# Last stage of a two-layer latent-attention and convolution backbone: the squares' sum moved to VectorE, the loads moved between the stores

## The chip, the core and the metric

The kernel runs on one core of a Trainium2 chip. The core has TensorE (matrix products into PSUM), VectorE and ScalarE (element-wise work), GpSimd, and SyncE, whose instruction stream only issues the DMA transfers here. In the rows they are PE (PEld for its weight loads), DVE, ACT, POOL and SP. The metric is the device time of one execution in microseconds, the median over several. All arithmetic is float32, with matrix products built from split high and low parts.

## The reference, cut to what matters

Two layers work on 2048 tokens of width 1024: an attention layer, then a convolution layer. The stage of this change computes the end of the second layer. `u` is the output of the depthwise convolution, `g` the gate path, `x` the stream before the layer:

```python
def layer_norm(x, g, b):
    mu = jnp.mean(xf, axis=-1, keepdims=True)
    var = jnp.mean(jnp.square(xf - mu), axis=-1, keepdims=True)
    y = (xf - mu) * lax.rsqrt(var + EPS)
    return y * g + b
...
    u = jax.nn.silu(layer_norm(u, g_ln, b_ln)) * jax.nn.silu(g)
    return u @ w_o
...
    x = x + gate_x * rms_norm(yx, g_post[i])
```

The mean and the variance run over the 1024 channels of each token.

## The kernel before, in words

The program is a row of stages: the projections of the first layer, its attention, its output, the projections and the convolution of the second layer, and last `conv_out`, from line 1762. Only `conv_out` is touched. It begins at about 2995 us of the profiled span and ends the program.

**Tiles.** `conv_out` handles the 2048 tokens as NB = 8 blocks of W = 256. A block lies with channels on the 128 partitions: KD = 8 groups of 128 channels, so `z` holds 128 x 8 x 256 numbers for it, in two halves of HK = 4 groups (1024 elements per partition each). `z` (the convolution's output) and `gt` (the silu of the gate) have two slots, `r` = 0 and 1; block number 2i + r uses slot r. The loops are written as a first pass (i = 0), a hardware loop (i = 1, 2) and a last pass (i = 3), each with two blocks.

**What a block goes through.** SyncE loads z and gt from HBM (`load_zg`, L1809, four transfers of 512 KB, issued at L1813). GpSimd adds the eight channel groups to one (`sums`, L2044 to L2046: 1024, 512, 256 elements wide). TensorE multiplies this with a matrix of ones, which sums over the partitions and gives each partition the result (`mean_sum`, L1998, one matmul that the chip runs as two instructions, since it is plain float32). ScalarE scales it to `mu` (L1857), VectorE subtracts it in two halves (`centre`, L1933), ScalarE squares the two halves into `sq` (L1861). TensorE sums the squares over channels: eight plain float32 matmuls with the ones, accumulated in `pvar` (`var_sum`, L2004, 16 instructions). ScalarE takes the root (L90), VectorE the reciprocal (L1938) and multiplies (`normalise`, L1942), ScalarE applies the silu by group (`silu_part`, L1876), GpSimd multiplies with the gate (`gate`, L2053), ScalarE rounds to the high part (`high`, L1885), VectorE takes the rest (`low`, L1949). TensorE then multiplies with the output weights: for each of two tiles of 128 tokens (u = 0, 1) and each of two halves of the output width (h = 0, 1) 24 matmuls of 512 columns (`split3`, L95 to L97). For each u, ScalarE sums the squares of the result (`stat`, L1892) and takes a root (L90), and VectorE forms the output (`residual`, L1955 reciprocal, L1957 from PSUM, L1963 adding `x`). SyncE stores it (L1845).

**The order of the work** is written out by hand, one order for each engine, and an engine takes its instructions strictly in this order. For block b (with n = b + 1 the next one):

- TensorE: group u0 h0, `var_sum(n)`, group u0 h1, group u1 h0, `mean_sum(b + 2)`, group u1 h1.
- ScalarE: `root(n)`, `silu_part(n)`, `stat(b, 0)`, `high(n)`, `mean(b + 2)` (scale, then both halves of the squares), `stat(b, 1)`.
- VectorE: `normalise(n)`, `residual(b, 0)`, `low(n)`, `centre(b + 2)`, `residual(b, 1)`.
- GpSimd: `sums(b + 2)`, `gate(n)`.
- SyncE: wait for `gate(b)`, `load_zg(b + 2)`, then for u = 0 and 1: wait for the output, store it, load the x of block n.

Ahead of the loop stand the first blocks' steps, mixed with the splitting of the eight weight groups (`weights_high`, `weights_low`, L1969). GpSimd there does `sums(0)`, `sums(1)`, `gate(0)`. `Chain` (L63) issues an instruction and waits for it on the same engine before the next.

Of the kernel before, what the change touches and what calls it, by code (L numbers as in the profile page):

```python
# [1756 lines left out]
def conv_out(nc, net):  # L1757
# [10 lines left out]
    with nc.cleanup_on_exit(), ExitStack() as st:  # L1768
# [17 lines left out]
        s_w, s_z, s_gt = net.sems("co_w_in", WR), net.sems("co_z_in", 2), net.sems("co_gt_in", 2)  # L1786
        s_x, s_st = net.sems("co_x_in", 2), net.sems("co_stored", 2)
        (s_const, s_whi, s_wlo, s_mean, s_mu, s_zc, s_sq, s_var, s_zn, s_v, s_vg, s_vhi, s_vlo, s_y, s_ss, s_tmp,
         s_out, s_rt, s_rs, s_mr, s_rr, s_zsum, s_add) = (net.sem("co_" + n) for n in (
             "const", "whi", "wlo", "mean", "mu", "zc", "sq", "var", "zn", "v", "vg", "vhi", "vlo", "y", "ss",  # L1790
             "tmp", "out", "rt", "rs", "mr", "rr", "zsum", "add"))
        block = st.enter_context(nc.Block())

        def loop(eng, body):

            body(0, True, False)
            with eng.Fori(1, NB // 2 - 1) as i:
                body(i, False, False)
            body(NB // 2 - 1, False, True)

        def nxt(i, r):
            return (i, 1) if r == 0 else (i + 1, 0)
# [6 lines left out]
        def load_zg(sp, i, r):  # L1809
            for dst, src, sem in ((z, net.z_phases, s_z), (gt, net.gate1, s_gt)):  # L1810
                for half in range(2):
                    g = slice(half * KD // 2, (half + 1) * KD // 2)
                    sp.dma_start(dst[:, r, g], src[g, :, bass.ds(i * 2 + r, 1), :].rearrange("g p a n -> p (g a) n")  # L1813
                                 ).then_inc(sem[r], 16)

        def rows(dram, i, r, u):

            return dram.rearrange("(n s) d -> s n d", s=PHASES)[bass.ds(i * 2 + r, 1), u * P:(u + 1) * P, :].rearrange(
                "a n d -> (a n) d")

        @block.sync
        def _(sp):
            def load_x(i, r, u):
                sp.dma_start(xt[:, u], rows(net.x1, i, r, u)).then_inc(s_x[u], 16)

            load_zg(sp, 0, 0)
            for dst, src in ((gln[:], net.g_ln), (bln[:], net.b_ln), (gp[:], net.gp_flat[1:2, :].to_broadcast([P, D]))):
                sp.dma_start(dst, src).then_inc(s_const, 16)
            for k in range(KD):
                if k >= WR:  # L1830
                    sp.wait_ge(s_wlo, k - WR + 1)
                sp.dma_start(wst[:, k % WR], net.w_o1[:, k]).then_inc(s_w[k % WR], 16)
            load_zg(sp, 0, 1)
            for u in range(TB):
                load_x(0, 0, u)

            def body(i, first, last):
                for r in range(2):
                    if not last:

                        sp.wait_ge(s_vg, i * 4 + 2 * (r + 1))
                        load_zg(sp, i + 1, r)
                    for u in range(TB):
                        sp.wait_ge(s_out, i * 4 + (2 * r + u + 1))
                        sp.dma_start(rows(net.out, i, r, u), ob[:, u]).then_inc(s_st[u], 16)  # L1845
                        if not (last and r):
                            load_x(*nxt(i, r), u)

            loop(sp, body)
            for u in range(2):  # L1850
                sp.wait_ge(s_st[u], 16 * NB)

        @block.scalar
        def _(act):
            def mean(i, r):
                act.wait_ge(s_mean, i * 2 + (r + 1))
                nc.scalar.activation(mu[:], pmu[:, 0:W], ACT.Copy, scale=1.0 / D).then_inc(s_mu, 1)  # L1857
                for half in range(2):
                    k = slice(half * HK, (half + 1) * HK)
                    act.wait_ge(s_zc, i * 4 + (2 * r + half + 1))  # L1860
                    nc.scalar.activation(sq[:, k], z[:, r, k], ACT.Square).then_inc(s_sq, 1)  # L1861

            def root(i, r):
                act.wait_ge(s_var, i * 2 + (r + 1))
                if not static(i, r) or r:
                    act.wait_ge(s_zn, i * 4 + 2 * r)
                root_mean(nc, net, rs[:], pvar[:, 0:W], D).then_inc(s_rt, 1)

            def silu_part(i, r):

                if not static(i, r) or r:
                    act.wait_ge(s_vlo, i * 4 + 2 * r)
                for k in range(KD):
                    if k % HK == 0:
                        act.wait_ge(s_zn, i * 4 + (2 * r + k // HK + 1))
                    nc.scalar.activation(v[:, k], z[:, r, k], ACT.Silu,  # L1876
                                         scale=gln[:, k:k + 1], bias=bln[:, k:k + 1]).then_inc(s_v, 1)

            def high(i, r):
                if not static(i, r):  # L1880
                    act.wait_ge(s_y, i * 4 + 2 * (r - 1))
                for half in range(2):
                    k = slice(half * HK, (half + 1) * HK)
                    act.wait_ge(s_vg, i * 4 + (2 * r + half + 1))
                    nc.scalar.activation(vhi[:, r, k], v[:, k], ACT.Copy).then_inc(s_vhi, 1)  # L1885

            def stat(i, r, u):
                s = 2 * r + u
                act.wait_ge(s_y, i * 4 + (s + 1))
                if not isinstance(i, int) or i:  # L1890
                    act.wait_ge(s_tmp, i * 4 + (s - 3))
                nc.scalar.activation(junk[:], ps[:, u], ACT.Square, accum_out=ss[:, s:s + 1]).then_inc(s_ss, 1)  # L1892
                act.wait_ge(s_ss, i * 4 + (s + 1))
                root_mean(nc, net, rr[:, s:s + 1], ss[:, s:s + 1], D).then_inc(s_mr, 1)

            act.wait_ge(s_const, 48)
            def weights_high(first, last):
                for k in range(first, last):
                    act.wait_ge(s_w[k % WR], 16 * (k // WR + 1))
                    nc.scalar.activation(whi[:, k], wst[:, k % WR], ACT.Copy).then_inc(s_whi, 1)  # L1900

            mean(0, 0)
            weights_high(0, 3)
            root(0, 0)
            weights_high(3, 5)
            silu_part(0, 0)
            high(0, 0)
            weights_high(5, KD)
            mean(0, 1)

            def body(i, first, last):
                for r in range(2):
                    n = None if last and r else nxt(i, r)
                    if n:
                        root(*n)
                        silu_part(*n)
                    stat(i, r, 0)
                    if n:
                        high(*n)
                    if not last:  # L1920
                        mean(i + 1, r)
                    stat(i, r, 1)

            loop(act, body)

        @block.vector
        def _(dve):
            def centre(i, r):
                dve.wait_ge(s_mu, i * 2 + (r + 1))
                dve.wait_ge(s_z[r], i * 32 + 32)  # L1930
                for half in range(2):
                    k = slice(half * HK, (half + 1) * HK)
                    nc.vector.tensor_tensor(z[:, r, k], z[:, r, k], mu[:].unsqueeze(1).to_broadcast([P, HK, W]),  # L1933
                                            ALU.subtract).then_inc(s_zc, 1)

            def normalise(i, r):
                dve.wait_ge(s_rt, i * 2 + (r + 1))
                nc.vector.reciprocal(rs[:], rs[:]).then_inc(s_rs, 1)  # L1938
                dve.wait_ge(s_rs, i * 2 + (r + 1))
                for half in range(2):  # L1940
                    k = slice(half * HK, (half + 1) * HK)
                    nc.vector.tensor_tensor(z[:, r, k], z[:, r, k], rs[:].unsqueeze(1).to_broadcast([P, HK, W]),  # L1942
                                            ALU.mult).then_inc(s_zn, 1)
# [26 lines left out]
                                            ALU.subtract).then_inc(s_wlo, 1)  # L1970

            centre(0, 0)
            weights_low(0, 3)
            normalise(0, 0)
            weights_low(3, 5)
            low(0, 0)
            weights_low(5, KD)
            centre(0, 1)

            def body(i, first, last):  # L1980
                for r in range(2):
                    n = None if last and r else nxt(i, r)
                    if n:
                        normalise(*n)
                    residual(i, r, 0)
                    if n:
                        low(*n)
                    if not last:
                        centre(i + 1, r)
                    residual(i, r, 1)  # L1990

            loop(dve, body)

        @block.tensor
        def _(pe):
# [2 lines left out]
                nc.tensor.matmul(pmu[:, 0:W], net.ones[:], zsum[:, 0], start=True, stop=True).then_inc(s_mean, 1)  # L1998

            def var_sum(i, r):  # L2000
                for k in range(KD):
                    if k % HK == 0:
                        pe.wait_ge(s_sq, i * 4 + (2 * r + k // HK + 1))
                    mm = nc.tensor.matmul(pvar[:, 0:W], net.ones[:], sq[:, k], start=(k == 0), stop=(k == KD - 1))  # L2004
                mm.then_inc(s_var, 1)

            mean_sum(0, 0)
            var_sum(0, 0)
# [185 lines left out]
```

## Time and profile before

| | us |
|---|---|
| median of 3 runs | 3262.49 |
| lowest and highest run | 3260.82, 3264.07 |
| the profiled execution's own time | 3262.19 |
| its span, from the first to the last instruction | 3260.2 |
| TensorE busy in the span | 3001.7 (92%) |
| VectorE, ScalarE, GpSimd busy | 1757.5, 1422.4, 431.0 |
| mean granted TensorE clock, share of full speed | 0.972 |

The profiled execution stands 0.3 us below the median. The busy shares are of the whole program; `conv_out` is its last 265 us, and an instruction of it is told by a name that begins with `co_`. Times of instructions are counted from the span's start. In a timeline row the columns are start, duration, engine, line, operation, output and inputs, shape, and, in brackets, the idle time of the engine before it with what ended it. Instructions of the same kind that follow each other stand as one row with their count.

### The profile page before, as it was taken

The page shows a single profiled execution, that of the slowest core. Times are in us where ns is not written, and L with a number is a line of the kernel's source. Part 1 is how long each engine was busy: PE and PEld are TensorE (multiplying, and loading weights), DVE is VectorE, ACT ScalarE, POOL GpSimd, SP SyncE. Part 2 cuts the span into 40 slices and gives each one's busy share as a digit, 9 for nine tenths or more (in the row PEclk, how much of TensorE's full clock was granted, in tenths as well). Part 3 has the DMA queues.
Part 4 walks back from the last instruction along what each step waited for, and adds up shares of the span by engine and source line. Part 5 has one row for each costly group of instructions (what it writes and reads, how often), then busy time and mean ns, then how long its engine had stood idle before and what let it go on. Part 6 is the DMA issues. An engine that isn't in the chain of part 4 may idle for free. (4 is left out here: it accounts for less than half of the span.)

```text
span 3260.2 us, 44295 instructions
## 1 busy us (share of the span) xinstructions
PE 3001.7 (92%) x15091; PEld 2495.0 (77%) x15091; DVE 1757.5 (54%) x2927; ACT 1422.4 (44%) x2971; POOL 431.0 (13%) x285
## 2 busy tenths in 40 slices
PE   2999999699999999999999998996899999997798
PEld 2878878588888878787878886784688888886677
DVE  6654554366766666767676765435233323333554
ACT  3554545356555655555555554325111111112543
POOL 1000000010111111110111110003011111112331
PEclk9999999899999999999999999997899999998899
DMA  6546455511112121211111100533222222213443
GB/s 219 182 158 228 147 178 182 174 51 44 51 33 69 40 70 40 69 36 44 50 55 54 40 27 29 203 127 123 71 70 70 65 68 73 70 54 125 134 155 103
DMA packets 217944, 308.07 MB, mean 94 GB/s; under 512 B 81008, under 2 KB 142720, under 8 KB 216576
## 3 DMA queue, kind: packets, MB, share of 16 engines
q1 hardware_dynamic: 213120, 296.98, 28.0%
q10 hardware_dynamic: 4608, 8.39, 0.7%
q8 instruction: 114, 1.87, 0.2%
q14 instruction: 102, 0.84, 0.1%
HBM read 213.94 MB, written 91.37 MB: 94 GB/s over the span
## 5 line engine op out<-in xcount | busy, mean ns | idle before, releaser
L1086 ACT ACTIVATE at_prob<-at_S,at_nmax 128x512 f32<-128x512 f32 (+1 forms) x640 | 411.4, 659 | 371.6 <-DVE at_nmax L1200 367.8
L1223 DVE TENSOR_TENSOR at_ptlo<-at_T,at_pthi 128x512 fp32r<-128x512 f32 x576 | 396.7, 689 | 319.4 <-ACT at_pthi L1102 318.3
L1102 ACT ACTIVATE at_pthi<-at_T 128x512 fp32r<-128x512 f32 x576 | 349.2, 609 | 225.4 <-PE at_T L972 225.4
L1189 DVE TENSOR_REDUCE at_mx<-at_S 128x1 f32<-128x512 f32 (+1 forms) x640 | 393.6, 630 | 84.2 <-PE at_S L946 77.4
L972 PE MATMUL at_T<-ident,at_prob 128*128 128x128 f32 x2304 | 345.8, 272 | 3.2 <-DVE at_ptlo L1223 3.2
L972 PEld LDWEIGHTS at_T<-ident,at_prob 128*128 128x128 f32 x2304 | 278.3, 140 | 69.4 <-DVE at_ptlo L1223 16.6
L95 PE MATMUL ci_ps<-h1hi,ci_whi 128*128 128x512 f32 x768 | 300.1, 391 | 17.6 <-DVE ci_wlo L1651 17.6
L96 PE MATMUL ci_ps<-h1lo,ci_whi 128*128 128x512 f32 x768 | 299.8, 390 | 0.0
L97 PE MATMUL ci_ps<-h1hi,ci_wlo 128*128 128x512 f32 x768 | 299.7, 390 | 0.0
L941 PE MATMUL at_S<-at_khi,at_qhi 128*128 128x512 f32 (+1 forms) x640 | 249.7, 390 | 48.6 <-ACT at_prob L1086 25.8
L95 PE MATMUL at_O<-at_pthi,at_vhi 128*128 128x512 f32 x576 | 272.8, 474 | 0.6 <-DVE at_og L1232 0.5
L516 DVE TENSOR_TENSOR fr_wlo<-fr_w,fr_whi 128x1024 fp32r<-128x1024 f32 (+1 forms) x99 | 114.6, 1160 | 250.0 <-ACT fr_whi L388 249.9
L945 PE MATMUL at_S<-at_krhi,at_qr 128*128 128x512 f32 (+1 forms) x640 | 238.7, 373 | 0.0
L943 PE MATMUL at_S<-at_khi,at_qlo 128*128 128x512 f32 (+1 forms) x640 | 238.0, 372 | 0.0
L946 PE MATMUL at_S<-at_krlo,at_qr 128*128 128x512 f32 (+1 forms) x640 | 237.7, 371 | 0.0
L942 PE MATMUL at_S<-at_klo,at_qhi 128*128 128x512 f32 (+1 forms) x640 | 237.4, 371 | 0.0
L97 PE MATMUL at_O<-at_pthi,at_vlo 128*128 128x512 f32 x576 | 227.6, 395 | 0.0
L96 PE MATMUL at_O<-at_ptlo,at_vhi 128*128 128x512 f32 x576 | 227.5, 395 | 0.0
L1607 ACT ACTIVATE ci_sig<-ci_ps 128x512 f32<-128x512 f32 x64 | 38.3, 598 | 429.1 <-PE ci_ps L97 429.1
L1658 DVE TENSOR_TENSOR ci_ub<-ci_ps,ci_sig 128x512 f32<-128x512 f32 x32 | 35.0, 1094 | 330.5 <-PE ci_ps L97 330.5
L1317 POOL TENSOR_TENSOR at_gden<-at_den,at_gst 128x512 f32<-128x512 f32 x32 | 41.4, 1294 | 1196.9 <-ACT at_den L1102 1196.9
L1752 POOL TENSOR_TENSOR ci_blo<-ci_tlo,ci_mask 128x640 fp32r<-128x640 f32 x64 | 109.0, 1712 | 604.4 <-DVE ci_tlo L1675 417.2
(202 smaller groups left out, 6391.9 us busy)
## 6 DMA issues: line engine op xcount, KB each, us to landing
fr_w<-in_w_front SPq DMA_DIRECT2D x75, 512.0 KB, 4.1
at_wmod<-in_w_mod SPq DMA_DIRECT2D x32, 512.0 KB, 3.3
ci_w<-in_cv_w_in SPq DMA_DIRECT2D x24, 512.0 KB, 4.2
fr_w<-in_w_front SPq DMA_DIRECT2D x24, 384.0 KB, 3.9
values<-fr_ob SPq DMA_DIRECT2D x36, 256.0 KB, 2.9
at_kst<-k_nope SPq DMA_DIRECT2D x8, 1152.0 KB, 7.3
at_vst<-values SPq DMA_DIRECT2D x8, 1152.0 KB, 7.3
fr_x<-in_x SPq DMA_DIRECT2D x16, 512.0 KB, 6.6
```

What stands on the lines that cost most here:

```text
L95: nc.tensor.matmul(out, whi, xhi, start=first, stop=False)
L96: nc.tensor.matmul(out, whi, xlo, start=False, stop=False)
L97: return nc.tensor.matmul(out, wlo, xhi, start=False, stop=last)
L941: nc.tensor.matmul(out, qhi[:, r, q], khi[:, k], start=True, stop=False)
L943: nc.tensor.matmul(out, qlo[:, r, q], khi[:, k], start=False, stop=False)
L945: nc.tensor.matmul(out, qr[:, r, q], krhi[:, k], start=False, stop=False)
L946: nc.tensor.matmul(out, qr[:, r, q], krlo[:, k], start=False, stop=True).then_inc(s_qk, 1)
L972: mm = nc.tensor.transpose(out[:, i * P:(i + 1) * P], prob[:, j % 2, i, kt * P:(kt + 1) * P], net.ident[:])
L1086: nc.scalar.activation(prob[:, j % 2, i, k], S[:, c, 0:k.stop - k.start], ACT.Exp, scale=SCALE, bias=nmax[:, i % 2:i % 2 + 1], accum_out=l ...
L1102: nc.scalar.activation(dst, T[:, (n + SLOTS * j) % 2], ACT.Copy).then_inc(s_hi, 1)
L1189: nc.vector.tensor_reduce(mx[:, i % 2, c:c + 1], S[:, c, 0:k.stop - k.start], AXX, ALU.max).then_inc(s_mx, 1)
L1223: nc.vector.tensor_tensor(ptlo[:, kt % 3], T[:, (n + SLOTS * j) % 2], pthi[:, kt % 3].bitcast(F32), ALU.subtract).then_inc(s_lo, 1)
```

## The change

The sum of the squares over channel groups moves from TensorE to VectorE: a new function `square_sums` adds the eight groups of `sq` in place in three steps, and `var_sum` becomes one matmul on the result. VectorE does it at the end of a block's list, after `residual(b, 1)`, for block b + 2. ScalarE gets a wait for the variance matmul of the block before, ahead of squaring. In the weights' order, VectorE splits two groups ahead of `square_sums(0, 0)` instead of three.

SyncE's list is written out flat over the eight blocks. Block 2's z and gt are loaded ahead of all stores, once `gate(0)` is done. After the first store (u = 0) of block b, and the x load behind it, SyncE waits for `gate(b + 1)` and loads z and gt of block b + 3.

```diff
-            def body(i, first, last):
-                for r in range(2):
-                    if not last:
-
-                        sp.wait_ge(s_vg, i * 4 + 2 * (r + 1))
-                        load_zg(sp, i + 1, r)
-                    for u in range(TB):
-                        sp.wait_ge(s_out, i * 4 + (2 * r + u + 1))
-                        sp.dma_start(rows(net.out, i, r, u), ob[:, u]).then_inc(s_st[u], 16)
-                        if not (last and r):
-                            load_x(*nxt(i, r), u)
-
-            loop(sp, body)
+            sp.wait_ge(s_vg, 2)
+            load_zg(sp, 1, 0)
+            for b in range(NB):
+                i, r = b // 2, b % 2
+                for u in range(TB):
+                    sp.wait_ge(s_out, i * 4 + (2 * r + u + 1))
+                    sp.dma_start(rows(net.out, i, r, u), ob[:, u]).then_inc(s_st[u], 16)
+                    if b + 1 < NB:
+                        load_x(*nxt(i, r), u)
+                    if u == 0 and b + 3 < NB:
+                        sp.wait_ge(s_vg, 2 * (b + 2))
+                        load_zg(sp, (b + 3) // 2, (b + 3) % 2)
...
                     act.wait_ge(s_zc, i * 4 + (2 * r + half + 1))
+                    if half == 0 and not (static(i, r) and r == 0):
+                        act.wait_ge(s_var, i * 2 + r)
                     nc.scalar.activation(sq[:, k], z[:, r, k], ACT.Square).then_inc(s_sq, 1)
...
+            def square_sums(i, r):
+                dve.wait_ge(s_sq, i * 4 + (2 * r + 2))
+                link = Chain(dve, s_sqadd, i * 4 + 2 * r)
+                link(nc.vector.tensor_tensor(sq[:, 0:HK], sq[:, 0:HK], sq[:, HK:KD], ALU.add))
+                link(nc.vector.tensor_tensor(sq[:, 0:HK // 2], sq[:, 0:HK // 2], sq[:, HK // 2:HK], ALU.add))
+                nc.vector.tensor_tensor(sq[:, 0], sq[:, 0], sq[:, 1], ALU.add).then_inc(s_sqsum, 1)
...
             centre(0, 0)
-            weights_low(0, 3)
+            weights_low(0, 2)
+            square_sums(0, 0)
+            weights_low(2, 3)
             normalise(0, 0)
             weights_low(3, 5)
             low(0, 0)
             weights_low(5, KD)
             centre(0, 1)
+            square_sums(0, 1)
...
                     residual(i, r, 1)
+                    if not last:
+                        square_sums(i + 1, r)
...
             def var_sum(i, r):
-                for k in range(KD):
-                    if k % HK == 0:
-                        pe.wait_ge(s_sq, i * 4 + (2 * r + k // HK + 1))
-                    mm = nc.tensor.matmul(pvar[:, 0:W], net.ones[:], sq[:, k], start=(k == 0), stop=(k == KD - 1))
-                mm.then_inc(s_var, 1)
+                pe.wait_ge(s_sqsum, i * 2 + (r + 1))
+                nc.tensor.matmul(pvar[:, 0:W], net.ones[:], sq[:, 0], start=True, stop=True).then_inc(s_var, 1)
```

## Rows read from the trace of the kernel before

**Rows 1.** Busy time by window: length, busy and instructions per engine, clock, DMA share, GB/s

```profile
3040.40:3210.40 170.00, 159.74 (x686) 130.29 (x685) 95.64 (x77) 86.04 (x133) 58.01 (x30) 0.98 0.40 130
3141.00:3143.00 2.00, 2.00 (x7) 1.52 (x6) 1.90 (x2) 1.06 (x1) 2.00 (x2) 0.50 0.00 0
```

**Rows 2.** Timeline of TensorE around the first and the last variance sum of the loop

```profile
3040.47 3.61 PE L2004 MATMUL co_pvar<-co_sq,ones 128*128 128x256 f32 x16
3043.74 0.58 PE L95 MATMUL co_ps<-co_whi,co_vhi 128*128 128x512 f32 x1
...
3210.41 0.38 PE L2004 MATMUL co_pvar<-co_sq,ones 128*128 128x256 f32 x1
```

**Rows 3.** The chain that ended last, one block's turn: start, duration, what

```profile
3127.56 6.87 DMA co_z<-z_phases
...
3134.59 2.39 POOL co_zsum L2044
...
3147.05 2.37 DVE co_z L1933 x2
...
3151.53 0.30 ACT co_rr L90
...
3153.37 1.24 DVE co_ob L1963
```

**Rows 4.** Timeline of ScalarE, roots and silus of two blocks

```profile
3097.80 0.47 ACT L90 ACTIVATE co_rs<-co_pvar,eps 128x256 f32<-128x256 f32 x1 [3.45 <-PE co_pvar L2004]
...
3101.36 4.05 ACT L1876 ACTIVATE co_v<-co_z,co_bln,co_gln 128x256 f32<-128x256 f32 x8 [1.78 <-DVE co_z L1942]
...
3126.18 0.47 ACT L90 ACTIVATE co_rs<-co_pvar,eps 128x256 f32<-128x256 f32 x1 [3.41 <-PE co_pvar L2004]
...
3131.07 4.05 ACT L1876 ACTIVATE co_v<-co_z,co_bln,co_gln 128x256 f32<-128x256 f32 x8
...
3137.44 0.29 ACT L90 ACTIVATE co_rr<-co_ss,eps 128x1 f32<-128x1 f32 x1
```

**Rows 5.** Groups by line, VectorE in the first stage: count, busy, mean ns

```profile
L528 DVE TENSOR_TENSOR fr_hlo<-fr_tmp,fr_hhi 128x512 fp32r<-128x512 f32 x32 | 22.1, 692 | 1.1
```

**Rows 6.** Timeline, GpSimd and VectorE at work together in block 3

```profile
3139.07 2.38 POOL L2053 TENSOR_TENSOR co_v<-co_v,co_gt 128x1024 f32<-128x1024 f32 x1
...
3139.44 3.09 DVE L1963 TENSOR_TENSOR co_ob<-co_tmp,co_x 128x1024 f32<-128x1024 f32 x1 [0.19 <-DVE co_tmp L1957]
...
3141.41 3.37 POOL L2053 TENSOR_TENSOR co_v<-co_v,co_gt 128x1024 f32<-128x1024 f32 x1
```

**Rows 7.** Timeline of SyncE's queue between blocks 2 and 3

```profile
3125.71 0.36 SPq L1845 DMA_DIRECT2D out_x<-co_ob  x1
...
3126.86 0.52 SPq L1813 DMA_DIRECT2D co_z<-z_phases  x1
```

**Rows 8.** Timeline of GpSimd, the channel sums

```profile
3021.48 2.86 POOL L2044 TENSOR_TENSOR co_zsum<-co_z 128x1024 f32<-128x1024 f32 x1 [16.79 <-DMA co_z<-z_phases]
...
3038.32 3.03 POOL L2044 TENSOR_TENSOR co_zsum<-co_z 128x1024 f32<-128x1024 f32 x1 [7.24 <-DMA co_z<-z_phases]
...
3166.13 1.27 POOL L2045 TENSOR_TENSOR co_zsum<-co_zsum 128x512 f32<-128x512 f32 x1
3167.48 0.72 POOL L2046 TENSOR_TENSOR co_zsum<-co_zsum 128x256 f32<-128x256 f32 x1
```

**Rows 9.** Timeline of ScalarE: the root for block 0, the squares of block 1

```profile
3015.21 0.47 ACT L90 ACTIVATE co_rs<-co_pvar,eps 128x256 f32<-128x256 f32 x1 [1.07 <-PE co_pvar L2004]
...
3038.00 2.20 ACT L1861 ACTIVATE co_sq<-co_z 128x1024 f32<-128x1024 f32 x2 [2.72 <-DVE co_z L1933]
```

**Rows 10.** Timeline of TensorE: pairs of the mean's matmul after idle time

```profile
3004.74 1.22 PE L1998 MATMUL co_pmu<-co_zsum,ones 128*128 128x256 f32 x2 [13.17 <-POOL co_zsum L2046]
...
3139.17 0.70 PE L1998 MATMUL co_pmu<-co_zsum,ones 128*128 128x256 f32 x2 [2.12 <-POOL co_zsum L2046]
```

More of the change, by code:

```diff
@@ L1788, in conv_out @@
         (s_const, s_whi, s_wlo, s_mean, s_mu, s_zc, s_sq, s_var, s_zn, s_v, s_vg, s_vhi, s_vlo, s_y, s_ss, s_tmp,
-         s_out, s_rt, s_rs, s_mr, s_rr, s_zsum, s_add) = (net.sem("co_" + n) for n in (
+         s_out, s_rt, s_rs, s_mr, s_rr, s_zsum, s_add, s_sqadd, s_sqsum) = (net.sem("co_" + n) for n in (
              "const", "whi", "wlo", "mean", "mu", "zc", "sq", "var", "zn", "v", "vg", "vhi", "vlo", "y", "ss",
-             "tmp", "out", "rt", "rs", "mr", "rr", "zsum", "add"))
+             "tmp", "out", "rt", "rs", "mr", "rr", "zsum", "add", "sqadd", "sqsum"))
         block = st.enter_context(nc.Block())
```

## The prediction

> **What bounds the kernel now.** I read the windows of the stage first, then TensorE's timeline, then the chain of waits, then the timelines of the engines that the chain names.
>
> The windows show where TensorE stands [rows 1]. From the first variance sum of the loop to the last, it is busy 159.74 of 170.0 us. It is nearly the bound, but idle 10.3 us. TensorE's timeline gives the scale [rows 2]: the variance sum of block 1 begins at 3040.47, that of block 7 at 3210.41, so six turns take 169.9 us, 28.3 each. One sum holds TensorE 3.27 us (the next group starts at 3043.74).
>
> The chain of waits says why a turn is longer than its matmuls [rows 3]. The chain runs through no matmul: the second output of block 2 is stored, z of block 5 is loaded (6.87 us from 3127.56), GpSimd adds its channel groups (2.39 us and two smaller), then multiplies with the gate, VectorE centres at 3147.05, and the turn closes with the second output of block 3, from 3153.37. So the load that waits for both stores is what stretches a turn, and TensorE waits for the mean's input, 2.12 us in one case [rows 10].
>
> **The change, part by part.**
>
> *The loads.* Each load leaves SyncE one output earlier, so z arrives some 12 us sooner (the first output's addition in block 3 ends at 3142.5 [rows 6], the second's at 3154.6 [rows 3]), and this chain is cut. SyncE's four issues now stand between the two stores; the second store's output comes about 10 us after the first, and the first issue takes 0.52 us [rows 7], so they cost it nothing. The wait for `gate(b + 1)` ahead of them ends before the first store (worked out below), so neither the second store nor the x load queued behind it is late. If only this were done, the next bound would be TensorE: four groups, the variance sum and the mean.
>
> *TensorE's part.* The 16 instructions become 2, 3.27 us become 0.35: 2.9 us less per block in TensorE's list.
>
> *ScalarE's added wait* asks for the variance of the block before. `root(n)` stands earlier in ScalarE's list and has waited for it already: nothing.
>
> *VectorE's part* is the one that decides. `square_sums(b + 2)` is last in the block's list, behind `residual(b, 1)`. TensorE needs it for `var_sum`, and all of the next block's chain follows from that matmul. So a new cycle closes: variance, root, normalise, silu, statistics, residual 0, low part, centre, squares, statistics, residual 1, adds, variance. I sum it from rows, starting with the matmul at 0:
>
> - The pair of matmuls until ScalarE starts: 0.70 at full clock and 1.22 at half, as the mean's pairs show [rows 10], and some 0.08 to the start; I take 1.0.
> - Root to first silu: 3126.18 to 3131.07 is 4.89 us. In blocks whose table load isn't behind the wait, it is 3097.80 to 3101.36, 3.56 us [rows 4]. Of the six turns, those for blocks 3 and 5 have the short form.
> - Silu to the root of statistics 0: 3131.07 to 3137.44, 6.37 us [rows 4].
> - That root to the output addition: 3151.53 to 3153.37, 1.84 us, then the addition 1.14 (two such instructions in a row take 2.37, so one advances 1.14 to 1.2) [rows 3].
> - Low part, two halves: 2.28. That puts the centring at 1.0 + 4.89 + 6.37 + 1.84 + 1.14 + 2.28 = 17.5.
> - Centring to the end of output 1: 3147.05 to 3154.61, 7.56 us [rows 3]. Sum 25.1. The squares and statistics 1 lie inside.
> - The three adds. The 1024-wide one as the 1.23 us of an output addition [rows 3], 0.69 for 512 elements [rows 5], and 0.42 for 256 by the slope between the two, with about 0.03 each for the waits of the chain: 2.4 us.
>
> The bare cycle is 27.5 us, or 26.2 with the short form. TensorE's own list needs only 0.35 + 0.35 + 96 x 0.229 = 22.7 us (after the last variance sum seven groups of 24 fill the 38.42 us of the last window [rows 1], 0.229 each). So TensorE idles; removing its work buys nothing, and VectorE with ScalarE becomes the bound at nearly the turn of now.
>
> *What collides with the adds.* GpSimd and VectorE exclude each other here. GpSimd's gate runs 3139.07 to 3141.45; the output addition started at 3139.44 takes 3.09 us where it takes 1.24 alone, that is, the rest of the gate and then its own time. The second gate, started at 3141.41, takes 3.37 where the first took 2.38, which is the addition's 1.1 [rows 6]. GpSimd's sum stretches in the same way, 2.39 alone [rows 3] against 2.86 and 3.03 beside VectorE [rows 8]. The Trainium skill, SBUF — State Buffer, section on the two separate sides, says the same of these two: a VectorE instruction with two SBUF inputs and a GpSimd one take a shared port pair in turn, for the whole instruction. By that rule the narrow instructions would exclude each other as well, for their whole length, and a meeting would cost all of GpSimd's 4.4 us.
>
> And it is. The first output is done at 17.5 - 2.28 = 15.2, its store issues then, z's load 1.15 us later (3125.71 to 3126.86 [rows 7]), and GpSimd's sum starts 7.7 us after the issue (3126.86 to 3134.59 [rows 3, 7]): at 24.1. Output addition 1 starts at 25.1 - 1.2 = 23.9. (The gates end near 5.9 + 2.2 + 2 x 2.4 = 12.9, before the store, as said above.) So the sums, 2.39 + 1.27 + 0.72 = 4.4 us [rows 3, 8], meet the addition and the three adds, and since both sides are chains of dependent instructions they alternate: VectorE's adds end later by nearly all of GpSimd's time. The rows show this for wide instructions alone; where only the wide sum is in the way, it is 2.4. The bounds are 0 (no meeting) and 4.4. I take 4.3, since the two small sums of GpSimd differ from the wide one in nothing but length; with 2.4 the time below would be 5 x 1.9 = 9.5 us less, 3272. With the short form both shift alike. It happens in the five turns in which a load is running; the sixth has none.
>
> **The sum.** Turns: 3 x 31.8 + 2 x 30.5 + 27.5 = 183.9, against 169.9: +14.0. The first variance: squares of block 1 end at 3040.2 [rows 9], GpSimd is in a sum until 3041.35 [rows 8], then the adds and the rest of the sums alternate: 1.2 + 1.3 + 0.7 + 0.7 + 0.4, to 3045.6, against 3040.47: +5.1. The opening: the variance of block 0 comes about 2 us later (root now at 3015.21 [rows 9]), which moves VectorE's split of weight groups 3 and 4 over GpSimd's sum of block 1 at 3021.48 [rows 8]; that sum waits one split (1.1) and the next split delays it once more, about +1.6, in exchange for a slack of 5 us in the silus. Behind the last variance: -2.9. TensorE resumes there after some 3 us of idling; after the 2.12 us one [rows 10] it ran a stretch at 0.50, that is 1.2 of 2.4 GHz [rows 1], and lost about 8 matmuls' extra 0.2 us: +1.9. In the other turns its slack takes this. Total 14.0 + 5.1 + 1.6 - 2.9 + 1.9 = +19.7 on the profiled execution's 3262.19: 3281.9. The median is 0.3 above it, which is inside my rounding: **3282**.
>
> **Rivals.**
>
> *No meeting, or the two share.* If z lands later or earlier than the adds, or GpSimd gets ahead, the turns are 27.5 and 26.2: 4 x 27.5 + 2 x 26.2 = 162.4, -7.5. The first variance then costs +2.4 and the opening up to 1.6: -7.5 + 2.4 + 1.6 - 2.9 + 1.9 = -4.5, so 3258. For it: a shift of 4 us in z suffices. Against: the load's time varied by less than 1 us, and both start points hang on the same output. Taken half, it gives 3270.
>
> *The change does what it looks like (the other side).* TensorE remains the bound, because VectorE's adds are ready when it reaches `var_sum`. Then a turn is 22.7 to 25 us; at 25 the six turns save 19.9 and with the last sum's -2.9 and the opening's +1.6 the time is near 3241. It decides where the cycle above is shorter than TensorE's list; I can't see 3 us too much in it. For it: VectorE is busy 95.64 of 170 [rows 1].
>
> *The clock stays at half after each idle stretch.* A first group at half takes 24 x 0.43 = 10.3 instead of 5.5. Then the statistics wait for TensorE at 1.3 + 10.3 = 11.6 instead of starting at 1.0 + 4.89 + 4.05 = 9.9 (eight silus take 4.05 [rows 4]): 1.7 to 3 us per turn, 6 x 2.1 = 13 more, 3295. The one stretch at half seen lasted about 4 us, which speaks against it.
>
> *The loads alone take effect*, and the adds hide behind other waits: this is the second rival with the adds' cost in place of the matmuls', and is inside its chance.
>
> **How the numbers follow.** The forecast, with a meeting of half to full size, has 0.66: slower. No meeting has 0.18, falling on both sides of -0.2% and of zero, mostly within. The rival on the other side has 0.07. The clock has 0.09. A measurement of this kernel can tell 0.2%, 6.5 us, from no change. Faster by over that: 0.07 + 0.04 = 0.11. Within: 0.14, with 0.01 of the weaker meetings, 0.15. Slower: 0.74. The range runs from the no-meeting case's upper side to the clock's, 3260 to 3295, leaving out about 0.2.
>
> **What would show it.** Right: `square_sums` in VectorE's timeline with 2 to 3 us for each add where the bare one takes 1.2; TensorE idle 5 us or more before L2004 and no longer before L1998; turns of about 31 us in TensorE's variance sums, the last one shorter by 4. The chain would run through VectorE and ScalarE with no z load. Wrong: turns of 28 or less, TensorE busy without a gap, z's sums before 20 or after 28 us from the variance matmul.

## The result, and the profile after

The changed kernel takes 3279.4 us (median of 5 runs, 3276.7 to 3281.3) against 3262.5 before (5 runs, 3260.8 to 3264.7): 1.0049 of the time before, with a 95% interval of 1.0036 to 1.0062. It is slower by 16.9 us, outside the 6.5 us that a measurement of this kernel can tell. The forecast was 3282, 3260 to 3295.

Earlier stages end some us sooner or later from one run to the next, so the stage is compared by its own length: from the first mean matmul to the last matmul. It was 247.4 us (3004.74 to 3252.13) and is 264.0 (3005.14 to 3269.10). All of the loss is here.

The windows over the six turns from the first variance sum to the last, columns as in [rows 1]:

```profile
3046.80:3228.70 181.90, 150.89 (x600) 121.99 (x600) 115.04 (x97) 84.05 (x132) 59.35 (x27) 0.89 0.38 124
```

TensorE has less to do, 150.9 us for 159.7 [rows 1], and the turns take 181.8 us for 169.9. Its idle time grew from 10 to 31 us, and its mean granted clock fell from 0.98 to 0.89. VectorE's busy time rose from 95.6 to 115.0.

TensorE's timeline at the fourth and the seventh variance sum:

```profile
3139.38 1.22 PE L2015 MATMUL co_pvar<-co_sq,ones 128*128 128x256 f32 x2 [5.17 <-DVE co_sq L1942]
...
3228.70 0.70 PE L2015 MATMUL co_pvar<-co_sq,ones 128*128 128x256 f32 x2 [2.66 <-DVE co_sq L1942]
```

Where the sum of block 1 followed the last group without a gap [rows 2], TensorE now waits for the last of VectorE's adds (L1942) at every block: 5.0, 5.8, 6.0, 5.2, 6.1, 5.2 and 2.7 us. The pair of matmuls takes 1.22 us after the six long waits and 0.70 after the last one. The granted clock says why: 0.50 (1.2 GHz) from 3046.88 to 3052.00, behind the first wait, and 0.99 in the 0.9 us from 3228.70. Behind that last pair the clock falls too, to 0.63 on average from 3228.70 to 3232.00.

The view of waits over the same six turns, in total us, times, longest:

```profile
POOL co_zsum L2054 <- DMA co_z<-z_phases: 57.7, 5, 11.8
ACT co_rs L90 <- PE co_pvar L2015: 54.5, 6, 10.0
...
PE co_pvar L2015 <- DVE co_sq L1942: 35.9, 7, 6.1
```

There is no wait of TensorE for the mean's input left, where [rows 10] had 2.12 us in one turn. The moved loads did their part. ScalarE's squares wait for VectorE's centring alone, so the wait added ahead of them costs nothing.

The chain that ended last, over one turn:

```profile
3130.96 1.30 DVE co_tmp L1965
3132.28 0.06 DVE co_ob L1971
...
3133.42 3.39 DVE co_sq L1940
3136.83 1.65 DVE co_sq L1941
3138.50 0.84 DVE co_sq L1942
3139.38 1.23 PE co_pvar L2015 x2
3140.64 0.48 ACT co_rs L90
3141.14 1.76 DVE co_rs L1946
3142.93 1.24 DVE co_z L1950
```

The load of z, 6.87 us of each turn in [rows 3], is gone from it. In its place stand the second output, the three adds, the matmul pair, the root. From 3133.42 to 3139.38 the adds take 6.0 us. VectorE's and GpSimd's timelines show why:

```profile
3132.28 1.22 DVE L1971 TENSOR_TENSOR co_ob<-co_tmp,co_x 128x1024 f32<-128x1024 f32 x1
3133.42 3.38 DVE L1940 TENSOR_TENSOR co_sq<-co_sq 128x1024 f32<-128x1024 f32 x1
3136.83 1.63 DVE L1941 TENSOR_TENSOR co_sq<-co_sq 128x512 f32<-128x512 f32 x1
3138.50 0.83 DVE L1942 TENSOR_TENSOR co_sq<-co_sq 128x256 f32<-128x256 f32 x1
```

```profile
3132.62 3.09 POOL L2054 TENSOR_TENSOR co_zsum<-co_z 128x1024 f32<-128x1024 f32 x1 [11.54 <-DMA co_z<-z_phases]
3135.79 2.13 POOL L2055 TENSOR_TENSOR co_zsum<-co_zsum 128x512 f32<-128x512 f32 x1
3138.00 1.05 POOL L2056 TENSOR_TENSOR co_zsum<-co_zsum 128x256 f32<-128x256 f32 x1
```

The output addition starts first and takes its bare 1.22, that is, its time with GpSimd idle. GpSimd's wide sum, started 0.34 us behind it, takes 3.09 instead of 2.39 [rows 3]. The first add waits that sum out, then GpSimd's second sum waits for the add, and so on by turns. Alone, in the stage's opening, the adds take 1.22, 0.69 and 0.42 us. So they pay 2.16 + 0.94 + 0.41 = 3.5 us in such a turn.

### The profile page after: what moved, and what is told of

It reads as the page before. It is cut to its first block and busy times, and to the rows that moved or that the text cites. A ratio compares the mean times of both kernels' runs of the same rounds, so it can differ in the third digit from the quotient of the medians.

```text
span 3277.2 us, 44037 instructions
## 1 busy us (share of the span) xinstructions
PE 2987.6 (91%) x14979; PEld 2481.6 (76%) x14979; DVE 1785.4 (54%) x2951; ACT 1421.6 (43%) x2971; POOL 438.0 (13%) x285
```

## The experiments

Each kernel ran beside the kernel before on the same chip. "Turns" are the six distances between variance sums in TensorE's timeline.

**loads_only.** The kernel before with SyncE's new list alone:

```diff
+            sp.wait_ge(s_vg, 2)
+            load_zg(sp, 1, 0)
+            for b in range(NB):
...
+                    if u == 0 and b + 3 < NB:
+                        sp.wait_ge(s_vg, 2 * (b + 2))
+                        load_zg(sp, (b + 3) // 2, (b + 3) % 2)
```

> Only the loads move; the variance stays eight matmuls on TensorE. My theory (the change loses by the adds at the end of VectorE's list, not by its loads): z comes about 12 us sooner, the chain through the load opens, and TensorE's own list of 25.7 us is the turn: 6 x 25.7 = 154 against 169.9, so 3245 to 3250, faster. Rival (the loads between the stores themselves delay a store or meet other transfers): 3262 or more.

Measured: 3245.5 us, 0.9947 (0.9931 to 0.9964). The turns are 25.7 us each. The window over them:

```profile
3041.00:3195.00 154.00, 154.00 (x685) 128.51 (x684) 83.00 (x77) 85.32 (x134) 57.20 (x30) 1.00 0.45 144
```

TensorE is busy in all 154.0 us, at full clock. The moved loads are a gain of some 17 us by themselves, and with them alone the kernel is bound by its matmuls.

**squares_only.** The changed kernel with SyncE's old list, so that only the adds are new:

```diff
+                        sp.wait_ge(s_vg, i * 4 + 2 * (r + 1))
+                        load_zg(sp, i + 1, r)
...
-                    if u == 0 and b + 3 < NB:
-                        sp.wait_ge(s_vg, 2 * (b + 2))
-                        load_zg(sp, (b + 3) // 2, (b + 3) % 2)
```

> Only the adds and the single matmul; the loads stay behind the second store. The z load then issues at about the time the adds run and lands 7.7 us later, so the two don't meet, but the chain through the load stays and the cycle through the adds is there too: turns of 28 to 29 us, 3265 to 3272. If the meeting of adds and GpSimd's sums were the only cost, 3262 or less; if the adds' place cost everything by itself, 3279 as with both parts.

Measured: 3269.9 us, 1.0025 (1.0015 to 1.0036), turns of 27.7 to 30.3, 174.0 in sum. VectorE's timeline has the adds bare:

```profile
3131.24 1.22 DVE L1941 TENSOR_TENSOR co_sq<-co_sq 128x1024 f32<-128x1024 f32 x1
3132.49 0.69 DVE L1942 TENSOR_TENSOR co_sq<-co_sq 128x512 f32<-128x512 f32 x1
3133.22 0.42 DVE L1943 TENSOR_TENSOR co_sq<-co_sq 128x256 f32<-128x256 f32 x1
```

They are bare in all six turns, and yet the kernel loses 7.6 us. GpSimd isn't wholly out of the way: in four of the turns it makes the first output's addition take 1.98 to 3.30 us, as it did in the kernel before [rows 6]. By its own length the stage is 9.6 us longer than before: 4.1 in the turns, 4.8 from the start of block 0 to the first variance sum, 1.5 ahead of that, and -0.8 behind the last sum.

The two parts don't add up: -17 and +8 give -9, and both together give +17. Each part is judged only by what bounds the turn beside it. With the new loads TensorE's list was the bound, and the adds replace it by a longer cycle. The new loads also bring GpSimd's sums to the adds; narrow_pool, below, prices that at some 20 of the 26 us.

**adds_first.** The whole change with two lines of VectorE's list exchanged:

```diff
-                    residual(i, r, 1)
                     if not last:
                         square_sums(i + 1, r)
+                    residual(i, r, 1)
```

> The whole change, but the adds stand ahead of the second residual in VectorE's list. My theory: they are done 2.7 us sooner by the order, and before GpSimd's sums begin, so the meeting goes as well: turns of 24 to 26 us, bounded by TensorE's list or near it, 3240 to 3250. Rival (TensorE's clock and idle time are the cause, or the adds are too dear anywhere in the list): no better than 3275.

Measured: 3246.8 us, 0.9956 (0.9939 to 0.9972), turns of 24.6 to 26.5. The same instructions in another place are worth some 32 us. In the turns the adds now run bare, ahead of GpSimd's sum, which is met by the output addition instead:

```profile
3144.62 0.42 DVE L1942 TENSOR_TENSOR co_sq<-co_sq 128x256 f32<-128x256 f32 x1
...
3146.47 2.60 DVE L1971 TENSOR_TENSOR co_ob<-co_tmp,co_x 128x1024 f32<-128x1024 f32 x1
3149.00 1.74 DVE L1946 RECIPROCAL co_rs<-co_rs 128x256 f32<-128x256 f32 x1
```

The root for that reciprocal started at 3145.92 and takes 0.47, so the reciprocal waits 2.6 us behind the second residual. The residual is on the path from the other side now. TensorE still waits 1.1 to 1.2 us for the adds at five of the six variance sums that end these turns, and up to 2.1 us for the low part.

**narrow_pool.** GpSimd's sums cut down, so that the adds meet next to nothing:

```diff
+                if not static(i, r):
+                    link(nc.gpsimd.tensor_tensor(zsum[:, 0, 0:32], z[:, r, 0, 0:32], z[:, r, 4, 0:32], ALU.add))
...
+                    return
```

> The whole change, but from block 2 on GpSimd adds only three pieces of 32 elements of z, so the mean of these blocks is wrong and GpSimd's sums take well under 1 us. My theory: each of the adds loses its wait of 2.2, 0.9 and 0.4 us in five turns and in the first variance, 6 x 3.5 = 21 less, minus about 0.5 us per turn for the short instructions: 3258 to 3264. Rival (the two only happen at the same time and the cycle is long by itself): 3275 to 3279.

Measured: 3258.1 us, 21.3 less than the changed kernel. The turns are 27.8, 27.8, 26.1, 27.8, 26.7 and 27.7, 163.8 in sum; the stage takes 243.9 us. VectorE's adds show nearly their bare time:

```profile
3125.83 1.27 DVE L1940 TENSOR_TENSOR co_sq<-co_sq 128x1024 f32<-128x1024 f32 x1
3127.14 0.69 DVE L1941 TENSOR_TENSOR co_sq<-co_sq 128x512 f32<-128x512 f32 x1
```

This is the price of the meeting: 18.0 us in the turns, and the rest of the stage's 20.1 us in the first variance. The four longer turns and the two shorter ones are the bare cycle of the prediction.

**narrow_adds.** The other side of the meeting, VectorE's adds cut to 32 elements:

```diff
-                link(nc.vector.tensor_tensor(sq[:, 0:HK], sq[:, 0:HK], sq[:, HK:KD], ALU.add))
...
+                link(nc.vector.tensor_tensor(sq[:, 0, 0:32], sq[:, 0, 0:32], sq[:, 4, 0:32], ALU.add))
...
```

> The whole change, but VectorE's three adds are 32 elements wide, so most of the squares are left out of the variance. It asks how the two engines meet. If one waits for the other's whole instruction, the first add, short as it is, waits out GpSimd's wide sum (2.4 us) and the next two wait for the 1.3 and the 0.7 us one, so the three still take some 4 to 4.6 us beside the 5.9 of before and turns fall by only 1.3 to 1.8: 3268 to 3272. If they share a rate, the short adds take 0.1 to 0.5 us and a turn falls by 5 us: near 3250.

Measured: 3263.4 us, 0.9999 (0.9990 to 1.0009), turns of 28.1 to 29.0 and a last one of 25.6. VectorE's and then GpSimd's timeline:

```profile
3130.32 2.35 DVE L1940 TENSOR_TENSOR co_sq<-co_sq 128x32 f32<-128x32 f32 x1
3132.71 1.30 DVE L1941 TENSOR_TENSOR co_sq<-co_sq 128x32 f32<-128x32 f32 x1
3134.05 0.19 DVE L1942 TENSOR_TENSOR co_sq<-co_sq 128x32 f32<-128x32 f32 x1
```

```profile
3129.55 3.08 POOL L2054 TENSOR_TENSOR co_zsum<-co_z 128x1024 f32<-128x1024 f32 x1 [11.56 <-DMA co_z<-z_phases]
3132.70 1.26 POOL L2055 TENSOR_TENSOR co_zsum<-co_zsum 128x512 f32<-128x512 f32 x1
```

An addition of 32 elements takes 2.35 us and ends with GpSimd's sum, the next 1.30 and ends with the next sum; one that met nothing takes 0.19. A shared rate can't do that, and its 3250 is far off. But the time missed my expectation too, 3268 to 3272. In this turn the third add slipped in ahead of GpSimd's last sum instead of waiting for it; in the other four the second slipped in (0.19 us) and the third waited out the middle sum (1.14). So the three took 3.7 to 3.9 us and not 4 to 4.6, and the first five turns fell by 2.2 us on average instead of 1.3 to 1.8. I had not allowed for the order of arrival changing with the lengths.

**one_add.** The adds ahead of the second residual, and only one of them; TensorE sums four groups:

```diff
+                nc.vector.tensor_tensor(sq[:, 0:HK], sq[:, 0:HK], sq[:, HK:KD], ALU.add).then_inc(s_sqsum, 1)
...
+                for k in range(HK):
+                    mm = nc.tensor.matmul(pvar[:, 0:W], net.ones[:], sq[:, k], start=(k == 0), stop=(k == HK - 1))
```

> Made to be faster than all: the adds ahead of the second residual, and only the first of them on VectorE; TensorE sums the remaining four groups (8 instructions, 1.7 us). TensorE's list is 24.1 us, VectorE's part 1.2 us shorter than with three adds, where turns were 25.3: turns of 24.1 to 24.6 and a cheaper opening, 3236 to 3242. If VectorE's adds were no longer what matters, it stays at 3245 to 3247.

Measured: 3242.0 us, 0.9933 (0.9916 to 0.9949). The first turn is 26.8 us, with a mean granted clock of 0.89 of full; the other five are 24.0 to 24.3, and TensorE is busy in all of them at full clock. The stage takes 228.4 us.

**late_residual.** The second residual moved behind the next block's normalise:

```diff
                     if n:
                         normalise(*n)
+                    if not (first and r == 0):
+                        residual(*((i, 0) if r else (i - 1, 1)), 1)
                     residual(i, r, 0)
...
-                    residual(i, r, 1)
```

> The whole change, but the second residual of a block goes behind the next block's normalise, into the time in which VectorE waits for the silus, and the adds end the list. The cycle through the adds loses the 2.7 us of the residual and the meeting; TensorE waits for PSUM some 1.4 us instead: turns of 24 to 24.8, 3238 to 3244. If the delayed PSUM release costs more than that, 3250 or more.

Measured: 3244.5 us, 0.9947 (0.9931 to 0.9964), turns of 23.9 to 24.9. TensorE waits 0.7 to 1.8 us per block for the PSUM that this residual reads (`DVE co_tmp`), as expected, and from the second variance sum of the turns on none for the adds. The time is 0.5 us above the expected 3238 to 3244, within the spread of its runs.

**two_adds.** From block 2 on, two adds ahead of the second residual and four instructions of TensorE for the variance; blocks 0 and 1 as in the kernel before:

```diff
+                groups = KD if static(i, r) else 2
+                if not static(i, r):
+                    pe.wait_ge(s_sqsum, i * 2 + (r - 1))
+                for k in range(groups):
...
```

> A version from what the runs so far show. From block 2 on VectorE does two adds (1024 and 512 elements) ahead of the second residual and TensorE sums two groups (4 instructions, 0.8 us); blocks 0 and 1 keep the eight matmuls, so the opening is as in the kernel before. With one add the sum was ready 1.4 us before TensorE came for it, so a second add of 0.7 us still fits and TensorE's list falls from 24.0 to 23.2 us: five turns of 23.2 after one of up to 25.7, 3228 to 3236. If VectorE becomes the bound again, turns of 24.5 and more and 3240 or more.

Measured: 3241.7 us, 0.9946 (0.9932 to 0.9959), turns of 24.1 to 26.0: a miss of the 3228 to 3236. TensorE waits for VectorE again, 3.0 us over the six turns for the adds and 3.0 for the low part. The output addition and GpSimd's sum in one turn:

```profile
3140.74 3.39 DVE L1971 TENSOR_TENSOR co_ob<-co_tmp,co_x 128x1024 f32<-128x1024 f32 x1
3144.05 1.74 DVE L1946 RECIPROCAL co_rs<-co_rs 128x256 f32<-128x256 f32 x1
```

```profile
3140.65 2.39 POOL L2057 TENSOR_TENSOR co_zsum<-co_z 128x1024 f32<-128x1024 f32 x1 [11.65 <-DMA co_z<-z_phases]
```

The second add delays the residual by 0.7 us, the addition arrives 0.09 us behind GpSimd's sum instead of ahead of it, and pays 2.2 us, which delays the reciprocal behind it.

**one_add_open.** One add again, and blocks 0 and 1 as in the kernel before:

```diff
+                groups = KD if static(i, r) else HK
...
```

> One add from block 2 on, blocks 0 and 1 with the eight matmuls on TensorE as before, otherwise as one_add. In the trace of two_adds the second residual's addition starts 0.1 us behind GpSimd's sum and waits it out (2.95 to 3.39 us); in one_add it starts 0.1 us ahead of it and takes 1.2. If that order of arrival decides, turns are 23.96 us as in one_add, and the opening of the kernel before saves 3 to 4 us: the stage, from its first mean matmul to its last matmul, takes 224 to 226 us against 228.4, and the run 3234 to 3240. If it doesn't, the turns are 24.5 or more and nothing is won.

Measured: 3234.4 us, 0.9919 (0.9906 to 0.9933), the fastest of all and 0.8% faster than the kernel before. The window over its six turns:

```profile
3040.20:3184.40 144.20, 144.19 (x637) 119.31 (x637) 94.78 (x81) 85.26 (x133) 61.77 (x28) 1.00 0.47 153
```

TensorE is busy throughout at full clock, the turns take 24.0 to 24.3 us, and all eleven output additions over them take 1.22 to 1.23 us. The stage takes 222.1 us, below the 224 to 226 expected, since the first turn wasn't longer than the others either.

## Why the prediction was right, point by point

**The bound now and the loads.** Right: the load chain of [rows 3] stretched the turn, and with it cut TensorE's own list is the turn, 25.7 us, as loads_only shows without a gap.

**VectorE's cycle.** Right, and its terms were close. The one turn without a meeting was put at 27.5 us and is 27.9; narrow_pool has 27.8 and, with the short form of the table load, 26.1 and 26.7 where 26.2 was summed. The adds are 1.22, 0.69 and 0.42 us as taken from [rows 3, 5] and the slope between them. Most of the small rest is the matmul pair, which I took at 1.0 us between the two rows of [rows 10] and which took 1.22 at the start of each of the six turns.

**The meeting.** Right in place, too large in size. I put output addition 1 at 23.9 us after the variance matmul and GpSimd's sum at 24.1. In the turn that begins at 3078.07, which has the long form that I summed, they start at 24.1 and 24.6; in the short-form turn from 3109.27 they start at 23.0 and 23.4, where the same sum gives 22.6 and 22.8. The price was 4.3 us per turn and is 3.5: the waits are 2.16, 0.94 and 0.41 us, where the sums met are 2.39, 1.26 and 0.72 long. I had charged the sums at their full durations. Each add pays 0.2 to 0.3 us less than that; how the two engines' instructions overlap at each change-over isn't shown. The sign that I gave, 2 to 3 us for each add, was loose: they take 3.4, 1.6 and 0.8. The exclusion that the prediction read from [rows 6, 8] holds for the narrow instructions too, which the rows alone left open. The Trainium skill, SBUF — State Buffer, section on the two separate sides, has whichever of the two starts first hold the shared port pair for the whole instruction while the other waits; the 2.35 us for 32 elements in narrow_adds agrees.

**The ledger**, forecast against measured:

| term | forecast us | measured us |
|---|---|---|
| six turns | +14.0 | 181.8 - 169.9 = +11.9 |
| start of block 0 to first variance | +5.1 | 12.79 - 8.25 = +4.5 |
| opening, first mean to block 0 | +1.6 | 28.95 - 27.48 = +1.5 |
| last variance to last matmul | -2.9 + 1.9 = -1.0 | 40.4 - 41.7 = -1.3 |
| sum | +19.7 | +16.6 |

The stage starts 0.4 us later in the profiled run, which makes the span's 17.0. What was mis-sized is the meeting's 4.3: the five turns at 3.5 are 4.0 us less, and the rest of the turns' terms give 1.9 back. Behind the last variance sum the clock's term, put at +1.9, is 1.6: the 41.7 and 40.4 us less the sum's own 3.27 and 0.35. So the forecast lies 2.6 us from the measured median partly because errors of either sign cancel.

**The rivals.** No meeting was priced at 3258; narrow_pool, which makes it so, runs at 3258.1. The other side, VectorE in time for TensorE and near 3241, was refuted in the changed kernel by TensorE's waits of 2.7 to 6.1 us. One exchange of two lines comes near it, with 3246.8 and waits of 1.2 us, and one_add and one_add_open bring it. The clock staying low for a whole group and delaying the statistics doesn't show: behind the variance sum at 3046.88 the matmuls are back at their full pace from 3052.1 on, TensorE's group ends near 3055.4 and ScalarE's silus only at 3057.1. In the turns TensorE's loss at half clock lies inside its own waits.

## What to carry to other kernels

Work taken from the busiest engine is no gain when its replacement stands last in another engine's list and the next step of everything hangs on it: sum the new cycle through all engines' lists, not one engine's load. Where VectorE adds two tensors in SBUF and GpSimd works beside it, put the short dependent additions where GpSimd is idle. Here a change of order was worth 32 us, and arriving 0.1 us too late cost an addition 2.2 us. When a change has two parts, time each alone: here one part was the gain and the other spent it twice.

## What the runs showed of the hardware that was not expected

Which of the two engines comes first decides who pays, down to differences of 0.1 us: the output addition took 1.22 us in one_add_open where it started 0.07 us ahead of GpSimd's sum (3089.03 and 3089.10), and 3.39 in two_adds where it started 0.09 behind it. In three of two_adds' six turns it was behind, and took 2.95 to 3.39. In the changed kernel's turns the engine that waited went next each time, so two chains of dependent instructions alternate one by one.

The time at which the stage begins, with nothing changed ahead of it, ranged over 8 us between the profiled runs (first mean matmul at 3001.6 to 3009.9 us). The cause wasn't looked for; for changes of 0.2% the stage's own length was the better measure.
